# Neighbourhood attention on one core: scores and transposes of two pairs of heads issued in groups

## What is computed

```python
def row_block(args):                       # one grid row of 64 query tokens, 4 rows in all
    q_r, r = args
    k_band, v_band = ...                   # 4 rows x 64 columns of keys and values
    bias = rpb_f[:, dr_idx[None, :, None], dc_idx[:, None, :]]
    bias = jnp.where(col_in[:, None, :], bias, -jnp.inf)          # 16 columns are in the window
    s_loc = jnp.einsum('bqhd,bikhd->bhqik', q_r, k_band).astype(jnp.float32) + bias
    s_ctx = jnp.einsum('bqhd,blhd->bhql', q_r, k_c).astype(jnp.float32)   # 256 context tokens
    s = jnp.concatenate([s_loc.reshape(b, nh, GRID_W, band), s_ctx], axis=-1)
    prob = jax.nn.softmax(s, axis=-1).astype(v.dtype)
    return p_loc @ v_band + p_ctx @ v_c                           # per head, written as einsums
```

## Time and profile before

| | us |
|---|---|
| median of 3 runs | 2625.88 (2624.85 to 2625.99) |
| profiled execution, its own time | 2627.89 |
| span in its profile | 2625.5 |
| TensorE busy | 2578.4 |
| VectorE busy | 1992.1 |
| ScalarE busy | 610.4 |
| attention stage, first scores in the loop to the gate matmuls | 85.15 |

### The profile page before, as it was taken

One profiled execution on the slowest core, in us unless ns is written; L12 is line 12 of the kernel. 1 busy time (PEld: TensorE's weight loads), 2 busy tenths in 40 slices (PEclk: granted clock), 3 DMA queues, 4 the chain that ended last, 5 costly groups with the idle time before them and its releaser, 6 DMA issues.

```text
span 2625.5 us, 31829 instructions
## 1 busy us (share of the span) xinstructions
PE 2578.4 (98%) x13052; PEld 2113.9 (81%) x13052; DVE 1992.1 (76%) x2296; ACT 610.4 (23%) x1288; POOL 137.2 (5%) x99
## 2 busy tenths in 40 slices
PE   6999999999999999999999999999999999999999
PEld 3788888888887876899788888788888888878887
DVE  4797796978656647887877888777687778978776
ACT  2122121311222138212210332410021023242101
POOL 0000000000002012200200002010000000100000
PEclk8999999999999999999999999999999999999999
DMA  7533242444544633555655545365565555444653
GB/s 272 176 131 109 97 145 75 134 160 160 176 147 142 197 86 76 178 196 177 202 179 171 187 159 189 113 198 180 176 194 185 182 179 182 144 145 161 201 183 120
DMA packets 252576, 424.53 MB, mean 162 GB/s; under 512 B 35584, under 2 KB 93376, under 8 KB 251920
## 3 DMA queue, kind: packets, MB, share of 16 engines
q1 hardware_dynamic: 248352, 410.09, 48.4%
q0 software_dynamic: 2560, 7.16, 0.9%
q10 hardware_dynamic: 1520, 5.25, 0.5%
HBM read 419.32 MB, written 3.15 MB: 161 GB/s over the span
## 4 chain that ended last, share of the span: by engine, by line
PE 91%; DVE 5%; ACT 2%; DMA 1%; issue 1%; ACTq 0%; POOL 0%; DVEq 0%
PE psum L511 86%; PE psum L525 3%; DVE wgt_lo L1812 1%; PE psum L859 1%; DVE wgt_hi L1810 1%; DMA raw<-ada_w 1%; ACT W L1238 1%; ACT L1238 0%; ACT xh L1238 0%; DVE xl L1833 0%; DVE W L2297 0%; ACT n_prob_b L1238 0%; DMA cst<-consts 0%; PE psum L671 0%; DVE xl L1821 0%
## 5 line engine op out<-in xcount | busy, mean ns | idle before, releaser
L1812 DVE TENSOR_TENSOR wgt_lo<-raw,wgt_hi 128x2048 fp32r<-128x2048 f32 (+1 forms) x332 | 752.7, 2267 | 11.4
L511 PE MATMUL psum<-wgt_hi,xh 128*128 128x512 f32 (+1 forms) x1744 | 682.6, 391 | 2.9 <-DVE wgt_lo L1812 2.0
L511 PE MATMUL psum<-wgt_hi,xl 128*128 128x512 f32 (+1 forms) x1744 | 675.9, 388 | 0.0
L511 PE MATMUL psum<-wgt_lo,xh 128*128 128x512 f32 (+1 forms) x1728 | 669.3, 387 | 0.0
L1810 DVE CAST wgt_hi<-raw 128x2048 fp32r<-128x2048 f32 (+1 forms) x332 | 403.6, 1216 | 129.7 <-PE psum L511 120.9
L511 PEld LDWEIGHTS psum<-wgt_hi,xh 128*128 128x128 f32 x1744 | 327.4, 188 | 73.9 <-issue 5.7
L511 PEld LDWEIGHTS psum<-wgt_hi,xl 128*128 128x128 f32 x1744 | 327.3, 188 | 66.3
L511 PEld LDWEIGHTS psum<-wgt_lo,xh 128*128 128x128 f32 x1728 | 324.6, 188 | 62.5
L511 PE MATMUL psum<-wgt_hi,yh 128*128 128x512 f32 x928 | 364.9, 393 | 1.5 <-DVE wgt_lo L1812 1.0
L511 PE MATMUL psum<-wgt_hi,yl 128*128 128x512 f32 x928 | 361.6, 390 | 0.0
L511 PE MATMUL psum<-wgt_lo,yh 128*128 128x512 f32 x928 | 361.4, 389 | 0.0
(11 more groups left out here) (240 smaller groups left out, 2215.2 us busy)
## 6 DMA issues: line engine op xcount, KB each, us to landing
raw<-mlp_w SPq DMA_DIRECT2D x64, 1024.0 KB, 5.4
raw<-w_in SPq DMA_DIRECT2D x60, 1024.0 KB, 5.1
raw<-ada_w SPq DMA_DIRECT2D x48, 1024.0 KB, 5.5
raw<-ffn_w_gate SPq DMA_DIRECT2D x40, 1024.0 KB, 5.1
raw<-ffn_w_up SPq DMA_DIRECT2D x40, 1024.0 KB, 5.1
raw<-ffn_w_down SPq DMA_DIRECT2D x40, 1024.0 KB, 5.1
raw<-ret_w_in SPq DMA_DIRECT2D x24, 1024.0 KB, 5.3
raw<-nat_w_in SPq DMA_DIRECT2D x12, 1024.0 KB, 5.3
```

The costliest lines, as they stand in the source:

```text
L511: return pe.matmul(o, l, r, start=start_, stop=stop, skip_group_check=True)
L1812: v.tensor_tensor(wgt_lo[:, s % RING, :size], r, wgt_hi[:, s % RING, :size], ALU.subtract).then_inc(split_done.sem, split_done.up())
```

## The change

The loop over n goes in steps of two. In each round TensorE issues the scores of pairs n and n + 1, then the transposes of pairs n - 2 and n - 1, then the values of pairs n - 4 and n - 3. Before, scores and transposes alternated pair by pair, with the values behind every second one. What is waited for by each instruction stays as it was.

```diff
-            for n in range(2, N_PAIRS + 3):
+            for n in range(2, N_PAIRS + 3, 2):
                 if n < N_PAIRS:
                     nat_scores(n)
+                    nat_scores(n + 1)
                 if n < N_PAIRS + 2:
                     nat_transposes(n - 2)
+                    nat_transposes(n - 1)
                 if n == 4:
                     pe.wait_ge(out_of(("nv", 1, 3)), emptied(("nv", 1, 3)))
-                if n >= 4 and n % 2 == 0:
+                if n >= 4:
                     nat_values((n - 4) // 2)
```

## The result

The changed kernel takes 2636.68 us, the median of 5 runs (2635.47 to 2637.17), beside 2625.88 (2624.85 to 2626.39) of the kernel before: a ratio of 1.0043, with a 95% interval of 1.0032 to 1.0053. It is slower by 10.8 us where 13.2 were forecast, and lies inside the range of 2635 to 2645.

What follows compares the result with a forecast made beforehand. TensorE was taken as the bound, with ScalarE close behind; after the change ScalarE's trip sets the pace: 2.82 + 87.43 + 8.08 = 98.33 us against 85.15, 13.2 longer, giving 2639.1 us, range 2635 to 2645.

Steps and rivals of the forecast that it cites:

- The trip: Attention stage: ScalarE's round from one first copy to the next sets the pace, 6.02 us, 6.47 with the inverses' spreading.
- The spreading: ScalarE's spreading of the inverses, every second round of the attention stage: charged at 0.45 us.
- A: The forecast as theory: ScalarE's round sets the pace, since the second scores stand between earlier exponentials and the first transposes.
- The bank wait: Second transposes wait for ScalarE's copy of the first ones' half: 0.32 us, 15 times, 4.8 us, hidden in the sum.
- The waits in front of S(n+1): TensorE's second scores of a round wait for the previous pair's exponentials to empty their banks: 0.96 and 0.15 us in turn.
- ScalarE's wait: ScalarE's waiting for TensorE's transposes in the attention stage rises from 9.2 to some 27 us in 15 waits of 1.8.
- The start: Stage's beginning: scores of pairs 2 and 3 at 2.12 us plus 0.70 to the first copy, 2.82 us.
- rival (a): Attention stage: scores of two pairs run side by side, making it faster by 11.9 us, 2614.0; chance 3%.
- Rival (c): TensorE's idle time lowers its clock once in each of 15 rounds: 25.5 us more, 2664.6; chance 8%.
- the prediction's own signs of being wrong: Trips of 5.4 or less with TensorE gapless, granted clock under 1.00 between 963 and 1061, or a later wait repaying it.
- The tail: Stage's end, from ScalarE's copies of pair 28 through the last values and inverse transposes: 8.08 us.
- The sum: Whole attention stage: 2.82 + 87.43 + 8.08 = 98.33 us against 85.15, 13.2 us longer.

Runs made afterwards that it cites:

- Undoing the exchange: Changed kernel with the first transposes put back between the two scores, values still behind both transposes: 2625.22 us beside 2625.56 of the kernel before.
- the added pieces: ScalarE's copy of odd pairs cut into four pieces: 2641.46 us in the changed kernel, 2625.27 in the kernel before (one run each).
- the added scores: Scores of even pairs from 2 on computed twice: 2637.97 us in the changed kernel, 2637.67 in the kernel before (one run each).
- the second profile of the changed kernel: The changed kernel run again unaltered: 2638.46 us (5 runs) beside 2625.41 of the kernel before, 1.0049.

## Why the prediction held, step by step

**The trip.** This is the term that decided, and it was right in kind and in size: 6.05 and 6.35 us against 6.02 and 6.47. The spreading had been charged from 992.74 to 993.19, its start to the start of an idle time; with a copy ready behind it, it costs 0.31 (982.14 to 982.45). Fourteen trips are 86.8 against 87.43. Undoing the exchange gave all of it back. Time added to ScalarE's list, or taken from it, came out in the trip and in nothing else, as A said, though the sizes written down for the added pieces and the added scores were too high.

**The bank wait.** 0.31 us by the starts of the rows, predicted 0.32, and hidden as predicted.

**The waits in front of S(n+1).** Predicted 0.96 and 0.15; by the starts they are 0.80 (1.86 - 1.06) and 0.13 (2.25 - 2 x 1.06). The first is shorter mainly because the spreading is.

**ScalarE's wait.** Predicted some 27 us in 15 waits of 1.8; 26.7 us in 17.

**The start: a step that failed.** Two S one behind the other and 0.70 were to make 2.82; it is 1.76. TensorE and ScalarE at the stage's start, two timelines of the changed kernel:

```profile
958.99 1.14 PE L511 MATMUL psum<-W 32*128 32x512 f32 x8
960.06 1.09 PE L859 MATMUL psum<-cst,n_prob_a 128*128 128x128 f32 x8
```

```profile
960.75 1.09 ACT L1240 ACTIVATE n_probT<-psum 128x512 f32<-128x512 f32 x2 [1.06 <-PE psum L859]
```

Eight matmuls of scores take 1.14 us, where four take 1.13: the scores of two pairs ran side by side. What rival (a) needs is real, and the sum's start should have used it. It pays once, 1.06 us, because the exponentials of pairs 0 and 1 are long over there (the last starts at 917.86); in every later round S(n+1) waits for E(n-1), as the prediction said of that rival. The Trainium skill (TensorE: Matmul & The Clock Gate, The mechanism in Part 3), which has matmuls of different row groups overlap, agrees with this for all four groups.

**The clock: a rival that came true in small.** Rival (c) supposed a fall in each round; there were one to three in the stage, 0.66 to 1.8 us in all. A granted clock under 1.00 was also one of the prediction's own signs of being wrong, and it is 0.95; the price it foretold, 25.5 us, did not come. The argument from the one stretch that had left the clock alone was too strong. "A second HAM failure mode: psum-queue depth-cycling" on the same page of the Trainium skill tells of a kernel whose short idle times between groups of matmuls made the clock swing. The trace agrees that it can: here it swung once to three times in a stage, at 0.6 to 0.7 us a time.

**The tail.** Predicted 8.08. In the second profile of the changed kernel, which has no fall there, TensorE's end of the stage is:

```profile
1054.01 1.14 PE L859 MATMUL psum<-cst,n_prob_b 128*128 128x128 f32 x8 [0.73 <-ACT n_probT L1240]
1055.08 2.03 PE L511 MATMUL psum<-n_probT,W 128*32 128x128 f32 x64
...
1057.31 1.95 PE L511 MATMUL psum<-cst,mod 128*128 128x128 f32 x16
```

From ScalarE's copies of pair 28, at 1049.23, to the gate it is 8.08. The 0.88 in front of the last values is gone, as the prediction had it: the values of four pairs follow one another.

**The sum.** 98.33 was predicted for the stage and 98.46 measured. That is closer than the steps deserve: 1.06 too much at the start and 0.63 too much in the trips stand against 1.8 for the clock, which the sum did not have. The order alone cost 11.5 us (96.64 - 85.15) where 13.2 was forecast, and the falls made up the rest: that the stage came out right to 0.1 us is luck.

**From the stage to the time.** The stage grew by 13.3 us, the span of the profiled executions by 9.3 (2625.5 to 2634.8). The 4.0 between them lie ahead of the stage, which began at 962.94 before and at 958.99 after, in a part that the change doesn't touch. In the twelve profiles of before, after and the experiments the stage begins anywhere from 958.99 to 962.94, whatever the order (the changed kernel's three at 958.99 to 959.97, but kernels with the same lists up to there at up to 962.59); TensorE's waits for the first loads of `ada_w` are among what differs (6.6 us in the profile of before, 4.7 after). So the difference of two profiled executions is uncertain by up to 4 us here. The differences of 10.8, 13.05 and 9.6 us in time lie within that of the 12.2 to 13.3 us by which the stage grew in the three profiles of the changed kernel; no finer agreement is shown.

## What to carry to other kernels

Where two engines hand work back and forth in fixed order, add up the trip (from one item of the one engine to the same item of the next round) as well as each engine's busy time. ScalarE had 1 us free per round and TensorE's work didn't change, yet 1.06 us of scores put between two links of the trip made it 6.05 and 6.35 us, where TensorE alone had set 5.36 on average. An idle engine is no reserve when its idle time is its wait for the engine that it in turn holds up.

To find which engine bounds a stage, add a piece of work to one engine in both orders and compare stage lengths and trips in the trace, not only times, which differ by as much as 4 us for other reasons. Cutting one copy of ScalarE in pieces told it here: nothing in the old order, 0.18 us in every trip of the new. Choose work that cannot run beside its neighbour: half of the doubled scores could.

## What the runs showed of the hardware

- Scores of four row groups (32 partitions each, 512 columns, fp32) run side by side: eight matmuls in 1.14 us at the start of the changed kernel's stage, four in 1.13.
- Small operations on ScalarE cost by their starts 0.48 us for a copy of 512 columns from PSUM, 0.16 for one of 128 (four in 0.63), and 0.31 for the spreading to 256 columns.
- TensorE's clock was lowered to 0.5 for 3.4 us at a time, one to three times in the changed kernel's stage, at 0.5 to 0.7 us a time; in the order with the values between the transposes a fall cost 1.5 us.
